# Seven block products for eight in the output projections of a feed-forward's two middle groups

## What is computed

```python
def swiglu(h, w_gate, w_up, w_down):
    return (jax.nn.silu(h @ w_gate) * (h @ w_up)) @ w_down

x = x + 0.5 * swiglu(rms_norm(x, norm_g[layer, 0]), ffn_w_gate[layer, 0],
                     ffn_w_up[layer, 0], ffn_w_down[layer, 0])
```

## Time and profile before

| | |
|---|---|
| median of 3 runs | 2028.01 us (2027.02 to 2029.37) |
| profiled execution: span | 2027.1 us |
| TensorE busy | 2018.1 us, 13750 matmuls |
| VectorE busy | 1438.7 us (71%) |
| ScalarE busy | 812.6 us (40%) |
| GpSimd busy | 663.9 us (33%) |

### The profile page before, as it was taken

One profiled execution on the slowest core, in us unless ns is written; L12 is line 12 of the kernel. 1 busy time (PEld: TensorE's weight loads), 2 busy tenths in 40 slices (PEclk: granted clock), 3 DMA queues, 4 the chain that ended last, 5 costly groups with the idle time before them and its releaser, 6 DMA issues.

```text
span 2027.1 us, 34383 instructions
## 1 busy us (share of the span) xinstructions
PE 2018.1 (100%) x13750; PEld 1999.4 (99%) x13750; DVE 1438.7 (71%) x2287; ACT 812.6 (40%) x1362; POOL 663.9 (33%) x723
## 2 busy tenths in 40 slices
PE   9999999999999999999999999999999999999998
PEld 8999999999999999999999999999999999999998
DVE  5786675864766678667587688485777878576685
ACT  6442333443434434333345354242335544333343
POOL 2562442502000056244240354262421356243340
PEclk9999999999999999999999999999999999999999
DMA  6233232333222223322233123223242213323222
GB/s 160 73 86 93 66 99 69 84 90 96 66 63 64 73 65 87 88 79 80 73 100 100 53 72 98 77 66 94 71 127 68 77 45 84 96 71 94 73 58 84
DMA packets 312846, 165.23 MB, mean 82 GB/s; under 512 B 15539, under 2 KB 310271, under 8 KB 312688
## 3 DMA queue, kind: packets, MB, share of 16 engines
q1 hardware_dynamic: 307840, 157.31, 28.3%
q0 software_dynamic: 2672, 4.65, 1.0%
q10 hardware_dynamic: 2176, 1.07, 0.2%
HBM read 159.01 MB, written 4.00 MB: 80 GB/s over the span
## 4 chain that ended last, share of the span: by engine, by line
PE 98%; DMA 0%; DVE 0%; ACT 0%; ACTq 0%; issue 0%; DVEq 0%
PE psum L544 32%; PE psum L546 32%; PE psum L545 32%; PE psum L927 1%; PE psum L822 0%; DMA in_raw<-in_ffn_w_up 0%; PE psum L589 0%; PE psum L786 0%; PE psum L606 0%; PE psum L806 0%; PE psum L829 0%; PE psum L828 0%; PE psum L795 0%; PE psum L569 0%; DVE x L1501 0%; PE psum L559 0%
## 5 line engine op out<-in xcount | busy, mean ns | idle before, releaser
L544 PE MATMUL psum<-xg_hi,in_hi 128*128 128x320 f32 x1952 | 608.3, 312 | 1.5 <-DVE xg_lo L1457 0.7
L546 PE MATMUL psum<-xg_hi,in_lo 128*128 128x320 f32 x1952 | 603.2, 309 | 0.0
L545 PE MATMUL psum<-xg_lo,in_hi 128*128 128x320 f32 x1952 | 603.1, 309 | 0.0
L1957 POOL TENSOR_TENSOR sums<-in_raw 128x256 f32<-128x256 f32 x288 | 269.1, 954 | 695.5 <-DVE in_lo L1423 463.9
L544 PE MATMUL psum<-f_hi,f_out_hi 128*128 128x320 f32 x1408 | 435.8, 310 | 0.0
L546 PE MATMUL psum<-f_hi,f_out_lo 128*128 128x320 f32 x1408 | 435.1, 309 | 0.0
L545 PE MATMUL psum<-f_lo,f_out_hi 128*128 128x320 f32 x1408 | 435.1, 309 | 0.0
L544 PEld LDWEIGHTS psum<-xg_hi,in_hi 128*128 128x128 f32 x1952 | 366.5, 188 | 5.7 <-issue 3.0
L545 PEld LDWEIGHTS psum<-xg_lo,in_hi 128*128 128x128 f32 x1952 | 366.6, 188 | 0.2
L546 PEld LDWEIGHTS psum<-xg_hi,in_lo 128*128 128x128 f32 x1952 | 366.5, 188 | 0.0
L544 PE MATMUL psum<-mix_hi,in_hi 128*128 128x320 f32 x864 | 267.0, 309 | 0.0
(11 more groups left out here) (236 smaller groups left out, 2769.2 us busy)
## 6 DMA issues: line engine op xcount, KB each, us to landing
in_raw<-in_ffn_w_gate SPq DMA_DIRECT2D x87, 512.0 KB, 4.0
in_raw<-in_ffn_w_up SPq DMA_DIRECT2D x86, 512.0 KB, 5.3
out_raw<-in_ffn_w_down SPq DMA_DIRECT2D x96, 384.0 KB, 3.4
out_raw<-in_ffn_w_down SPq DMA_DIRECT2D x32, 256.0 KB, 2.9
in_raw<-in_mix_w_in SPq DMA_DIRECT2D x14, 512.0 KB, 4.6
out<-y_nat SPq DMA_DIRECT2D x5, 512.0 KB, 3.4
in_raw<-in_mix_w_in SPq DMA_DIRECT2D x8, 256.0 KB, 4.4
out_raw<-in_mix_w_out SPq DMA_DIRECT2D x16, 128.0 KB, 2.9
```

The source lines that it names most:

```text
L544: pe.matmul(dst, w_hi, v_hi, start=first, stop=False)
L545: pe.matmul(dst, w_hi, v_lo, start=False, stop=False)
L546: return pe.matmul(dst, w_lo, v_hi, start=False, stop=last)
L1957: last = pool.tensor_tensor(to[:, part], a[:, part], b[:, part], op)
```

## The change

The out stages of groups 1 and 2 of each feed-forward no longer use plain units. Four pairs of output blocks (`PAIRS`) by two token halves, with the six hidden blocks taken as three pairs, are made by seven products of three k-steps each, so 7 x 3 x 3 matmuls a pair of output blocks, where four units of 6 x 3 stood. The products are added in place: slots 0, 2, 3 and 5 run on in one bank (4 or 5), slots 1 and 6 in banks 6 and 7, slot 4 in bank 7, and VectorE adds the bank to a quarter of `x` after each product (`fold`), 28 times a group. A product that runs on in a bank waits for the fold before it.

The weights of these steps take the path of the in stage: loaded into `in_raw`, summed by GpSimd at 4 x 384 columns, split into the slots. All steps, in and out, stand in one list (`STEPS`), and the order of products, of splits and of folds is given by three lists. The three hidden combinations (slots 2, 3 and 5) need sums of hidden values: VectorE makes one more subtraction in `hidden_high` of each first chunk of a pair, then three differences (`hidden_sum`) and, after ScalarE's three high parts, three low parts (`hidden_sum_low`). For pairs 0 and 1 of a group these stand in the in stage at its chunks 2 and 4; for pair 2 they stand in the out stage.

Core of the diff:

```diff
+            def hidden_high(index, g, i):
+                fast = chunk_of(index, sum(GROUPS[:g]) + i)
+                lower, upper = temps(g, i)
+                dve.wait_ge(gate_done, 2 * fast + 2)
+                if g in SEVEN and i % 2 == 0:
+                    n = len(SEVEN) * 3 * index + 3 * SEVEN.index(g) + i // 2 + 1
+                    dve.tensor_tensor(upper, upper, t1[:, 1], ALU.mult).then_inc(upper_done, 1)
+                    dve.wait_ge(upper_done, n)
+                    dve.tensor_tensor(pair_mix[:, :], upper, lower, ALU.subtract).then_inc(hidden_done, 1)
+                else:
+                    dve.tensor_tensor(upper, upper, t1[:, 1], ALU.mult).then_inc(hidden_done, 1)
...
                 for g, gk in enumerate(GROUPS):
                     f0 = sum(GROUPS[:g])
                     for f in range(f0, f0 + gk) if g else ():
...
                         if i > 0:
-                            gate_high(s - 1)
-                            hidden_split(i - 1, 0, u - 1, 1)
-                            hidden_high(s - 1)
-                            weights_late(f)
-                            hidden_split(i - 1, 1, u, 0)
+                            gate_high(s - 1, fast - 1)
+                            hidden_split(i - 1, 0, u - 1, temps(g, i - 1)[0])
+                            hidden_high(index, g, i - 1)
+                            if g in SEVEN and i % 2 == 0:
+                                for t in range(3):
+                                    hidden_sum(index, g, i // 2 - 1, t)
+                            fast_low(s, 6, 7)
+                            upper_split(index, g, i - 1)
+                            if g in SEVEN and i % 2 == 0:
+                                for t in range(3):
+                                    hidden_sum_low(index, g, i // 2 - 1, t)
+                        elif g - 1 in SEVEN:
+                            fold(index, g - 1, PAIRS - 1, 5)
                         wait(dve, hidden_done, u - 1)
-                        gate_low(s)
...
+                        gate_low(s, fast)
+                        if i == 0 and g - 1 in SEVEN:
+                            fast_low(s, 4, 6)
+                            fast_low(s, 6, 7)
+                        ups(s, fast, u, lower, upper, early)
```

VectorE's list in the new out stage (TensorE's is `for slot in (0, 4, 1)`, then slots 2 and 6 in parts, then for each q the products 0(q), 3(q-1), 4(q), 1(q), 5(q-1), 2(q), 6(q)):

```diff
+            def fold_outputs(index, g):
+                s, last = step_of(index, g, GROUPS[g]), GROUPS[g] - 1
+                f = sum(GROUPS[:g]) + last
+                hidden_split(last, 0, 44 * index + 2 * f + 1, temps(g, last)[0])
+                gate_high(s - 1, chunk_of(index, f))
+                hidden_high(index, g, last)
+                hidden_sum(index, g, 2, 0)
+                hidden_sum(index, g, 2, 1)
+                fold(index, g, 0, 0)
+                hidden_sum_low(index, g, 2, 0)
+                fold(index, g, 0, 4)
+                fast_low(s, 6, 7)
+                upper_split(index, g, last)
+                hidden_sum(index, g, 2, 2)
+                fold(index, g, 0, 1)
+                fast_low(s + 1, 0, 1)
...
+                for q in range(1, PAIRS):
+                    fold(index, g, q, 0)
+                    fold(index, g, q - 1, 3)
+                    fast_low(s + q, 2, 4)
+                    fast_low(s + q, 6, 7)
+                    fold(index, g, q, 4)
+                    fold(index, g, q, 1)
+                    fast_low(s + q + 1, 0, 2)
+                    fold(index, g, q - 1, 5)
+                    fast_low(s + q, 5, 6)
+                    if q < PAIRS - 1:
+                        fast_low(s + q + 1, 4, 5)
+                    fold(index, g, q, 2)
+                    fold(index, g, q, 6)
+                fold(index, g, PAIRS - 1, 3)
+                fast_low(s + PAIRS, 2, 4)
```

GpSimd's sums no longer wait for the end of the group before a first chunk's weights:

```diff
-                    elif f in FIRST_CHUNKS:
-                        pool.wait_ge(hidden_lo, 44 * index + 2 * f)
...
+                    if s:
+                        pool.wait_ge(fast_split, max(split_at(s - 1, 2), split_at(s - 1, 3)))
```

More of the change, by code:

```diff
@@ L25 @@
 NEXT_TILES = {(0, 3): (0, 0), (1, 3): (0, 1), (2, 3): (1, 0), (3, 1): (1, 1)}
-FIRST_CHUNKS = [sum(GROUPS[:g]) for g in range(len(GROUPS))]
+PAIRS = KT // 2
+SEVEN = (1, 2)
 assert sum(GROUPS) == FT and max(GROUPS) == SLOTS
@@ L72, with product_order @@
 DVE_KEEPS = (3, 4, 7)
+STEPS = []
+for _g in range(1, len(GROUPS)):
+    _f = sum(GROUPS[:_g])
+    STEPS += [("in", _g, f) for f in range(_f, _f + GROUPS[_g])]
+    if _g in SEVEN:
+        STEPS += [("out", _g, q) for q in range(PAIRS)]
+N_STEPS = len(STEPS)
+OUT_BANK = {0: (4, 5), 2: (4, 5), 3: (4, 5), 5: (4, 5), 1: (6, 6), 4: (7, 7), 6: (7, 7)}
+def product_order():
+    order, held = [], []
+    for n, (kind, _, q) in enumerate(STEPS):
+        if kind == "in":
+            order += [(n, 0)] + held + [(n, slot) for slot in range(1, 7)]
+            held = []
+        elif q == 0:
+            order += [(n, slot) for slot in (0, 4, 1, 2, 6)]
+            held = [(n, 3), (n, 5)]
+        else:
+            order += [(n, 0), held[0], (n, 4), (n, 1), held[1], (n, 2), (n, 6)]
+            held = [(n, 3), (n, 5)]
+            if q == PAIRS - 1:
+                order.append(held.pop(0))
+    return order
@@ new lines, in split_order @@
+def split_order():
+    order = []
+    for n, (kind, _, q) in enumerate(STEPS):
+        if kind == "in":
+            if n == 0:
+                order += [(n, (0, 2)), (n, (2, 4)), (n, (4, 6)), (n, (6, 7))]
+            if n + 1 < N_STEPS:
+                order += [(n + 1, part) for part in ((0, 2), (2, 4), (4, 6), (6, 7))]
+        elif q == 0:
+            order += [(n + 1, (0, 1)), (n + 1, (4, 5)), (n + 1, (1, 2))]
+        else:
+            order += [(n, (2, 4)), (n, (6, 7)), (n + 1, (0, 2)), (n, (5, 6))]
+            order += [(n + 1, (4, 5))] if q < PAIRS - 1 else [(n + 1, part) for part in ((2, 4), (4, 6), (6, 7))]
+    return order
@@ new lines, in fold_order @@
+def fold_order():
+    order = [(0, slot) for slot in (0, 4, 1, 2, 6)]
+    for q in range(1, PAIRS):
+        order += [(q, 0), (q - 1, 3), (q, 4), (q, 1), (q - 1, 5), (q, 2), (q, 6)]
+    return order + [(PAIRS - 1, 3), (PAIRS - 1, 5)]
+PRODUCT_ORDER, SPLIT_ORDER, FOLD_ORDER = product_order(), split_order(), fold_order()
+PRODUCT_AT = {key: i + 1 for i, key in enumerate(PRODUCT_ORDER)}
+SPLIT_AT = {(n, slot): i + 1 for i, (n, part) in enumerate(SPLIT_ORDER) for slot in range(*part)}
+FOLD_AT = {key: i + 1 for i, key in enumerate(FOLD_ORDER)}
@@ new lines, with step_of, product_at, split_at @@
+assert len(PRODUCT_AT) == len(SPLIT_AT) == 7 * N_STEPS
+def step_of(index, g, i):
+    return N_STEPS * index + STEPS.index(("in", g, sum(GROUPS[:g]) + i) if i < GROUPS[g] else ("out", g, i - GROUPS[g]))
+def product_at(s, slot):
+    return len(PRODUCT_AT) * (s // N_STEPS) + PRODUCT_AT[s % N_STEPS, slot]
+def split_at(s, slot):
+    return len(SPLIT_ORDER) * (s // N_STEPS) + SPLIT_AT[s % N_STEPS, slot]
+def fold_at(index, g, q, slot):
+    return len(FOLD_ORDER) * (len(SEVEN) * index + SEVEN.index(g)) + FOLD_AT[q, slot]
@@ L75, in first_half_count, with sums_at, out_base @@
+def sums_at(index, g, pair, t):
+    return 3 * (len(SEVEN) * 3 * index + 3 * SEVEN.index(g) + pair) + t + 1
+def out_base(g):
+    return 0 if g == 0 else 1
 def first_half_count(m):
@@ L697, in fast_in @@
                     if p == 0:
[L698 to L703 removed]
+                        wait(pe, p1_done, fast)
+                    elif fast > 0:
+                        pe.wait_ge(evac_done, 7 * (fast - 1) + (1, 2, 3, 5, 6, 7)[p - 1])
+                    if p >= 4 and g == 1:
+                        wait(pe, x_updated, OUT_UNIT[FFN_PHASE[index]] + 16)
```

481 lines of the change are left out of this document (313 added, 168 removed).

## The result

| | before | after |
|---|---|---|
| median | 2027.95 us (4 runs, 2027.02 to 2029.37) | 2070.35 us (4 runs, 2070.13 to 2071.24) |
| ratio | | 1.0207, 95% interval 1.0193 to 1.0222 |
| profiled execution: span | 2027.1 us | 2068.3 us |

The changed kernel is slower by 42.4 us. The prediction said slower, 2091 us in a range of 2040 to 2130. The sign, the mechanism and the range held; the forecast was 20.7 us too high.

The account below looks back on a forecast made before the run. TensorE bounds the kernel before, VectorE after: 2027.1 - 42.2 for removed matmuls + 105.6 of stalls (7.2 + 6.0 = 13.2 us a group, eight groups) = 2090.5 span, 2091.4 us with 0.9 around it; range 2040 to 2130.

Parts of the forecast that it names:

- What bounds the kernel: Before the change TensorE bounds; VectorE's in-stage chunk of 12.48 us exceeds TensorE's 12.32, its 1.09 idle being no reserve.
- Removed, 42.2 us: Out stages of eight middle groups: 288 fewer matmuls at 0.1467 us each, all on the path.
- Chunks 2 and 4, 3.7 more each: In stage, VectorE: six added operations at 0.41, 0.24 for waits, two more collisions at 0.5 us.
- Odd chunks, 1.03 more each: In stage, VectorE, chunks 1, 3, 5: one added subtraction, 0.41 plus 0.12 wait plus 0.5 collision.
- Waits in the in stage, 7.2 a group: TensorE stalls once VectorE's lag passes 5.55 us: 1.45, 1.2, 3.86, then 1.2 less 0.5.
- Start of the out stage, 6.0 a group: VectorE's list there ends at 12.6 us, TensorE could be there at 6.6; stall 6.0, or 3.8 without collisions.
- Moved edits at nothing: Low parts moved behind the next group's first gate evacuation, some 1.8 us, fall where VectorE waits for TensorE.
- The loop over q at nothing: Out stage: VectorE's 8.5 us fits beside TensorE's 9.24; little or no stall, up to 0.5 us a q if not.
- Rival D: Loads or slot chain of the q loop don't fit: 0.5 to 1 us a q, 2110 us; chance 0.08.
- Rival A: VectorE's additions cost only their bare time, 2.7 and 0.53 us: 2046 us; chance 0.16.
- Rival B: Faster: VectorE absorbs the additions in the 1.09 us behind ScalarE each chunk, no added collision: 1994 us; chance 0.13.
- Rival C: TensorE's gaps lower the clock, one chunk a group at 1.2 GHz, 12.32 us more each: 2190 us at most; chance 0.04.

Follow-up runs that it names:

- the idle-operation experiment: The kernel before with idle VectorE operations placed where the change has its own in the in stages of groups 1 and 2: 2078.76 us, ratio 1.0254.
- Taking away the 1.09: The changed kernel with ScalarE's high part of slots (0,2) moved ahead of the SiLU, so VectorE skips that 1.09 us wait: 2039.18 us, ratio 1.0061.
- no collision: The changed kernel with GpSimd's weight sums replaced by constant writes that read nothing, output not the reference's: 1987.72 us, ratio 0.9803.
- the run with the filler: The changed kernel with 23 idle matmuls (3.4 us) ahead of product 0 of chunk 5 in groups 1 and 2: 2073.81 us, ratio 1.0226.

## Why the prediction was right or wrong

- **What bounds the kernel:** right. By stage VectorE's room was nearly nothing, and its additions became TensorE's waits; the idle-operation experiment shows that with the old out stage.
- **Removed, 42.2 us:** right. 13462 records as forecast, and the pace in the loop over q is whole (0.1467 us a matmul from 985 to 1011 us).
- **Chunks 2 and 4, 3.7 more each:** right, 16.0 - 12.48 = 3.5, with four of the six operations at about 1 us.
- **Odd chunks, 1.03 more each:** too dear by 0.6 at chunk 3. Measured 12.87 - 12.48 = 0.39, the bare operation. The step took the collision as added. But the subtraction pushes the last low part of the chunk (`f_lo`, 941.09) behind the end of GpSimd's third sum, and GpSimd's last sum comes later too, since it waits for VectorE's `in_lo` (941.31). So this `f_lo` takes 0.48 where the earlier trace rows had 1.03. The new collision took the place of an old one. Chunk 1 of group 2 did grow by 15.43 - 14.15 = 1.28, of which 0.88 is more than in group 1's chunk (moved edits, below): that the forecast's lag after chunk 1 comes out near the measured one there is luck.
- **Waits in the in stage, 7.2 a group:** measured 5.0 in group 1 and 5.9 in group 2. The places at chunks 3, 4 and 5 were right. The term of chunk 3 was 0.55 instead of 1.2 (a stall of 0.55 is 12.87 - 12.32), the 3.86 was 3.65, and the 0.7 ahead of the out stage didn't come: chunk 5 takes 12.0 on VectorE, not 13.5.
- **Start of the out stage, 6.0 a group:** too dear. VectorE's list from slots (0,2) to the last of these is 984.11 - 972.15 = 12.0, not 12.6. And the forecast gave TensorE no lead, while (0,2) was ready at 972.15 and TensorE, after 84 matmuls from 960.79, could be there at 973.1: 0.95 more. 6.0 - 0.6 - 0.95 = 4.4, as where the clock didn't fall: 2.40 + 1.28 + 0.37 + 0.33. With the fall 2.9 of it shows as waiting and 1.5 as slower matmuls.
- **Moved edits at nothing:** not quite. Group 2's wait at chunk 3 is 0.9 more than group 1's, and its chunk 1 is 15.43 us on VectorE for group 1's 14.55, as much. Its first chunk follows a new out stage, and has the two low parts that were moved behind its gate evacuation; that these make the 0.9 fits the rows but wasn't tried by itself.
- **The loop over q at nothing:** right. It fits, without a wait. Just behind it, at product 3 of the last pair, one wait of 0.25 to 0.8 a group is left, which the forecast didn't have; where it is 0.8, the matmul's row names the fold before it in the same bank. Rival D's price wasn't paid.
- **Rival A** (bare additions, 2046) fell in the even chunks, where the rows show collisions, and held at chunk 3. **Rival B** (faster, 1994) named the wrong room. Taking away the 1.09 gave 31 us and no gain over before; the forecast's "no reserve" held for the order as it stood, not for another one on ScalarE. But its time was in reach: with no collision 1987.7, and with two sums moved 2015. That collisions could be moved by GpSimd's timing was not in the argument at all.
- **Rival C** (clock): the event came in seven of eight groups, and I gave it 0.04. Its price was not 12 us each but 1.5, and that was hidden. A granted clock below 1, named as a sign of a wrong forecast, was no such sign. Of the other signs, TensorE waited 71 us, not 105, and chunk 3 took 12.9 us, under the 13.5 to 16.

The sum, mended: 71.4 of waiting, and 12 for seven clock falls at 1.55, one of them of twice the length (8 x 1.55 = 12.4), less 42.2, is 41.6; the spans differ by 2068.3 - 2027.1 = 41.2. So 83.8 / 8 = 10.5 us a group stood where I had 13.2: 1.7 less in the in stage (5.5 for 7.2, mean of both groups), 1.6 less at the out stage's start (4.4 for 6.0), 0.5 more behind the loop over q.

## What to carry to other kernels

Before giving an engine more work, read its busy share in the stage that gets it and count its list against the bound's, from start to start: here an engine at 71% of the span had no room at all, its list being 0.16 us a chunk longer than TensorE's. VectorE's instructions with two SBUF inputs should not run beside GpSimd's reads: hold GpSimd back until VectorE evacuates PSUM or is idle anyway, which was worth 52 us here at the price of one wait (and nothing on the kernel before, where TensorE was the bound), and look at what a wait hides before removing it. Savings found one at a time can be the same saving.

## What the runs showed of the hardware

- At TensorE's gaps of about 3.65 us the granted clock fell to its lower level in seven of eight groups, from between 1.4 us before and 1.1 us after the gap's end, and stayed there for 3.4 us (6.8 in ffn0 group 2). In the line of the changed kernel behind ffn0 group 2's gap it is 0.50, with 14 matmuls; behind ffn3 group 1's gap of the same length it stayed at 1.00, with 23. I can't say what made that one differ. The Trainium skill, TensorE: Matmul & The Clock Gate, HAM oscillation, warns of gaps of this size, and the trace agrees in seven of eight. In the run with the filler the clock fell behind waits of 2.44 to 2.51 us as well at four places, and at four others with waits of 2.44 to 2.47 it didn't. That the loss can be free, when another engine is late just behind, is what the filler showed.

```profile
294.70:298.10 3.40, 3.40 (x14) 3.40 (x14) 3.30 (x6) 0.46 (x2) 1.36 (x2) 0.50 0.00 0
1765.60:1769.00 3.40, 3.35 (x23) 3.38 (x24) 3.26 (x7) 0.54 (x1) 0.90 (x2) 1.00 0.00 0
```

- GpSimd's writes of 256 columns (0.29 us each) left VectorE's two-input instructions at their undisturbed time; its reads of the same size cost one of 0.49 some 0.5 us.
